# Expert blocks of at most 64 rows: the rests of x and h beside their nearest halves as stationary columns, and changes at two stage boundaries

## The reference

```python
h = h + hybrid_mixer(rmsnorm(h), ...)            # retention, SSD, S5; then w_out
h = h + cross_attend(rmsnorm(h), mn, wq, wk, wv, wo)
h = h + hier_moe(rmsnorm(h), ...)

def hier_moe(xn, ...):
    gsel = argmax(xn @ w_rg + b_rg)              # one of 4 groups of 8 experts
    top_p, top_i = top_k(softmax(elog of that group), 2)
    gate = pg * top_p / sum(top_p)
    # the 4096 pairs (token, expert) are sorted by expert, each expert's padded
    # to blocks of 128 rows; a block is computed with its expert's weights:
    h = silu(xb @ w_gate[e]) * (xb @ w_up[e]);   y = h @ w_down[e]
    # and y * gate is added to the token's row
```

## Time and profile before

| | us |
|---|---|
| time, three runs | 2474.22, 2474.22, 2477.82 (median 2474.22) |
| the profiled execution | 2471.07 |
| its span, first to last instruction | 2469.2 |
| granted TensorE clock, mean of the span | 0.968 |
| mixer stages | 0 to 924 |
| cross attention and router | 924 to 1558 |
| experts: routing and block 0 | 1558 to 1626 |
| experts: blocks 1 to 46 | 1626 to 2405 |

### The profile page before, as it was taken

The page is one execution under the profiler, slowest core; times in us unless marked ns, Lnnn a source line. Parts: engine busy times, 40 slices in busy tenths (PEclk is TensorE's granted clock), DMA queues, the critical chain, the costliest instruction groups (busy, mean ns, idle before and its releaser), DMA issues. The chain is left out here.

```text
span 2469.2 us, 34866 instructions
## 1 busy us (share of the span) xinstructions
PE 2267.5 (92%) x11995; PEld 1292.0 (52%) x11996; DVE 1407.6 (57%) x2052; ACT 987.0 (40%) x1418; POOL 368.0 (15%) x272
## 2 busy tenths in 40 slices
PE   4999999999979989999999999399999999999990
PEld 2465565565658974555555555145445445445440
DVE  5566566565569854333333332677556777777753
ACT  4522432433321333222222222246456666666653
POOL 0022021121220000000000000003222222122222
PEclk9999999999989999999999999599999999999995
DMA  5201001002050134111110100379777899988957
GB/s 196 90 2 50 35 26 61 1 26 45 9 213 26 52 123 142 52 60 44 69 69 35 60 35 35 138 261 319 233 241 252 292 313 319 333 311 301 320 185 287
DMA packets 150950, 349.50 MB, mean 142 GB/s; under 512 B 28480, under 2 KB 33984, under 8 KB 150592
## 3 DMA queue, kind: packets, MB, share of 16 engines
q1 hardware_dynamic: 136016, 310.32, 34.5%
q0 software_dynamic: 13680, 33.58, 5.8%
q10 hardware_dynamic: 1152, 4.19, 0.4%
HBM read 303.48 MB, written 60.82 MB: 148 GB/s over the span
## 5 line engine op out<-in xcount | busy, mean ns | idle before, releaser
L111 PE MATMUL bankA<-main_room,hnT 128*128 128x512 f16 (+1 forms) x1536 | 303.2, 356 | 5.5 <-DVE main_room L609 5.5
L111 PE MATMUL bankE<-wg,xT 128*128 128x512 f16 x1128 | 255.6, 384 | 7.9 <-DVE xT L2484 7.4
L111 PE MATMUL bankE<-wd,hT 128*128 128x512 f16 x1128 | 251.1, 379 | 2.4 <-DVE hT L2489 2.4
L111 PE MATMUL bankE<-wu,xT 128*128 128x512 f16 x1128 | 251.1, 379 | 0.0
L111 PEld LDWEIGHTS bankA<-main_room,hnT 128*128 128x128 f16 x1536 | 151.7, 99 | 148.7 <-issue 7.3
L111 PEld LDWEIGHTS bankE<-wg,xT 128*128 128x128 f16 x1128 | 111.2, 99 | 144.9 <-issue 15.3
L111 PE MATMUL bankA<-hnT,main_room 128*128 128x512 f16 x768 | 170.4, 384 | 9.0 <-DVE hnT L585 9.0
L111 PEld LDWEIGHTS bankE<-wd,hT 128*128 128x128 f16 x1128 | 110.2, 98 | 125.7 <-issue 3.0
L111 PEld LDWEIGHTS bankE<-wu,xT 128*128 128x128 f16 x1128 | 110.3, 98 | 122.9
L2461 DVE SCALAR_TENSOR_TENSOR wg<-w_rows,wg 128x2048 f16<-128x2048 f32 x64 | 143.8, 2288 | 49.9 <-ACT wg L2232 49.9
L111 PE MATMUL bankC<-w_out_s,catT 128*128 128x512 f16 x768 | 169.4, 381 | 2.5 <-DVE w_probs L1861 2.5
(11 more groups left out here) (373 smaller groups left out, 3275.1 us busy)
## 6 DMA issues: line engine op xcount, KB each, us to landing
w_rows<-in_w_gate SPq DMA_DIRECT2D x64, 1024.0 KB, 5.8
w_rows<-in_w_up SPq DMA_DIRECT2D x64, 1024.0 KB
w_rows<-in_w_down SPq DMA_DIRECT2D x64, 1024.0 KB
x_room<-in_x SPq DMA_DIRECT2D x4, 2048.0 KB, 11.0
cat_t<-scratch_cat SPq DMA_DIRECT2D x16, 512.0 KB, 4.9
main_room<-in_x SPq DMA_DIRECT2D x16, 512.0 KB, 5.6
scratch_ybuf<-main_room SPq DMA_DIRECT2D x16, 512.0 KB, 2.6
out<-hf SPq DMA_DIRECT2D x16, 512.0 KB, 11.9
```

The costliest lines, as they stand in the source:

```text
L111: ins = pe.matmul(o, a[x][k], b[y][k], start=start and k == 0 and j == 0, stop=stop and k == n - 1 and j == 2)
```

## The change

**Short blocks.** `plan` gets a row of numbers (PL_HALF): for the last block of an expert, if it is not the expert's first, has at most 64 rows and is neither block 0 nor the last of all, its number among such blocks, else 0. It is computed by nine more operations on DVE in the routing. For such a block `x_rest` and `h_rest` write the rest of the 64 columns that hold tokens into columns 64 to 127 of the nearest half's tile. `short_products` then takes two products for each k tile: all 128 columns (nearest and rest) by the weights' nearest, whose rows 64 to 127 are the rest's share, and the 64 nearest columns by the weights' rest. That makes 16 for 24. The two halves of rows are added afterwards: ACT copies rows 64 to 127 of the bank (`gate_low`, `up_low`, `y_lows`), DVE adds them (`gate_sum`, `up_sum`, `y_sums`). All three engines read the new number in each step and branch on it; `last` keeps the whole form.

**Routing.** The clearing of `xr` and `again` moves from DVE to POOL. The counting matmuls are in f16 with their constants converted on ACT, and the counts no longer depend on the scan's whole output; ranks are waited for apart. The six operations on gates move behind the first lists.

**Cross boundary.** `probs_weights(0)` moves to the end of `s5_mixer`, and the PSUM banks `vbank` are kept across the boundary, so that `VB` names eight banks; the load of a head's rows waits for one head less.

```diff
+def short_products(pe, o, a, b):
+    both, nearest = a
+    n = len(both)
+    for k in range(n):
+        turn = (False, True) if k == n - 1 else (True, False)
+        for full in turn:
+            if full:
+                ins = pe.matmul(o, both[k], b[0][k], start=k == 0, stop=k == n - 1)
+            else:
+                pe.matmul(o[0:P // 2, :], nearest[k], b[1][k], start=False, stop=False)
+    return ins
...
@@ s5_mixer, behind its last products
+            pe.wait_ge(begun.w_co_ld[0], 16)
+            pe.wait_ge(memory.w_lo, 2 * KT)
+            head = big[:, 0:2 * D].rearrange("p (k n) -> p k n", k=2)
+            for m in range(MT):
+                for j in range(2):
+                    for e in range(2):
+                        ins = pe.matmul(memory.bank[2 * m + j], values_t[:, e, m * P:(m + 1) * P], head[:, e, j * 512:(j + 1) * 512], start=(e == 0), stop=(e == 1))
+                    ins.then_inc(begun.vw_first, 1)
...
             def head(h):
-                if h >= 2:
-                    sp.wait_ge(vw_done, 4 * (h - 1))
+                if h >= 3:
+                    sp.wait_ge(vw_done, 4 * (h - 2))
...
-            probs_weights(0)
+            probs_weights(1)
             pe.wait_ge(ld, 16)
+            pe.wait_ge(vw_lo, 4)
             turn_cat(0)
-            probs_weights(1)
             probs_weights(2)
             probs_weights(3)
...
+        def short_block(eng, b):
+            return eng.value_load(plan[0:1, bass.ds(PL_HALF + 1 + b, 1)], min_val=0, max_val=NE)
...
@@ ACT
             def step(b):
                 take_h(b - 1)
-                silu(b)
+                h = short_block(act, b)
+                with act.If(h < 1):
+                    silu(b)
+                with act.If(h > 0):
+                    gate_low(b, h)
+                    silu(b)
+                    up_low(b)
                 following(act, b, gates(b))
                 take_x(b + 1)
                 following(act, b, ups_downs(b))
-                take_y(b - 1)
+                h = short_block(act, b - 1)
+                with act.If(h < 1):
+                    take_y(b - 1)
+                with act.If(h > 0):
+                    y_lows(b - 1)
...
-            dve.memset(xr[:, :], 0.0).then_inc(x_clear, 1)
-            dve.memset(again[:, :, :], 1.0).then_inc(ready, 1)
-            dve.wait_ge(ready, 1)
-            dve.memset(again[:, :, 0:1], 0.0).then_inc(ready, 1)
-            dve.wait_ge(ready, 2)
...
@@ DVE
             def step(b):
-                h_rest(b - 1)
+                y_sums(b - 2)
+                by_rows(b - 1, h_rest)
+                h = short_block(dve, b)
+                with dve.If(h > 0):
+                    gate_sum(h)
                 following(dve, b, gate_rest)
-                product(b)
-                x_rest(b + 1)
+                with dve.If(h < 1):
+                    product(b)
+                with dve.If(h > 0):
+                    up_sum(h)
+                    product(b)
+                by_rows(b + 1, x_rest)
                 following(dve, b, up_down_rest)
...
-            pe.matmul(bank[5][:, :], lt, flat(both), start=True, stop=False)
+            pe.matmul(bank[5][:, :], lt_h[:, :], flat(both), start=True, stop=False)
+            pe.matmul(bank[6][:, 0:NE], ones_h[:, :], both[:, :, NCH - 1], start=True, stop=False)
             pe.wait_ge(summed, 2)
-            pe.matmul(bank[5][:, :], ones, flat(before), start=False, stop=True)
-            pe.matmul(bank[6][:, 0:NE], ones, cum[:, :, NCH - 1], start=True, stop=True).then_inc(cnt, 1)
+            pe.matmul(bank[6][:, 0:NE], ones_h[:, :], before[:, :, NCH - 1], start=False, stop=True).then_inc(cnt, 1)
+            pe.matmul(bank[5][:, :], ones_h[:, :], flat(before), start=False, stop=True).then_inc(ranked, 1)
...
-            def by_slot(b, do):
+            def by_slot(b, do, whole=False):
                 u = expert_of(pe, b)
+                h = 0 if whole else short_block(pe, b)
                 for slot in range(SLOTS):
                     with pe.If(u % 2 < 1 if slot == 0 else u % 2 > 0):
-                        do(slot, u)
+                        if whole:
+                            do(slot, u)
+                        else:
+                            with pe.If(h < 1):
+                                do(slot, u)
+                            with pe.If(h > 0):
+                                do(slot, u, short_products)
```

More of the change, by code:

```diff
@@ L2072, in experts @@
         e32, pos = work(2, NCH, NGR, EPG), work(2, NCH, NE)
-        both, before, cum, again = (work(0, NE, NCH) for n in range(4))
+        cum, again = (work(0, NE, NCH) for n in range(2))
+        both, before = (sb(n, [P, NE, NCH], F16) for n in ("both", "before"))
+        lt_h, ones_h = sb("lt_h", [P, P], F16), sb("ones_h", [P, P], F16)
         E8, t8, m8, O8 = (work(0, NCH, EPG) for n in range(4))
@@ L2077, in experts @@
         nblk, first_blk, end, used_e, rank, eq, t32, first_row = (work(0, NE) for n in range(8))
-        cols, turns_f, first_f = work(0, 6), work(0, 1), work(0, 1)
-        c_expert, c_u, c_block, c_split, c_more, c_half = (cols[:, i:i + 1] for i in range(6))
+        cols, turns_f, first_f = work(0, 8), work(0, 1), work(0, 1)
+        c_expert, c_u, c_block, c_split, c_more, c_half, c_short, c_nth = (cols[:, i:i + 1] for i in range(8))
+        short_e = work(0, NE)
         lt, ones, one = cst[:, K_LT:K_LT + P], cst[:, K_ONE:K_ONE + P], cst[:, K_ONE:K_ONE + NE]
@@ L2167, in _ @@
         def _(pool):
+            pool.memset(again[:, :, :], 1.0).then_inc(ready, 1)
+            pool.wait_ge(ready, 1)
+            pool.memset(again[:, :, 0:1], 0.0).then_inc(ready, 1)
+            pool.memset(xr[:, :], 0.0).then_inc(x_clear, 1)
             pool.wait_ge(x_clear, 1)
@@ L2222, in _ @@
         def _(act):
+            act.activation(lt_h[:, :], lt, ACT.Copy).then_inc(lt_ready, 1)
+            act.activation(ones_h[:, :], ones, ACT.Copy).then_inc(lt_ready, 1)
             act.wait_ge(r_steps, env["r_marks"][0])
@@ L2254, in silu, with gate_low, up_low, y_lows @@
                 act.activation(sg[:, :], bank[2][:, :], ACT.Silu, scale=1.0 / (W_SCALE * X_SCALE)).then_inc(sil, 1)
+            def gate_low(b, h):
+                act.wait_ge(gd, b + 1)
+                act.activation(low[:, :], bank[2][HB:P, :], ACT.Copy).then_inc(g_low, 1)
+                act.wait_ge(g_sum, h)
+            def up_low(b):
+                act.wait_ge(ud, b + 1)
+                act.activation(low[:, :], bank[3][HB:P, :], ACT.Copy).then_inc(u_low, 1)
+            def y_lows(b):
+                act.wait_ge(y_t, b * 2)
+                act.wait_ge(y_st, b * 16)
+                for j, done in enumerate((yl0, yl1)):
+                    act.wait_ge(yd, b * 2 + j + 1)
+                    act.activation(y_low[:, j * 512:(j + 1) * 512], bank[5 + j][HB:P, :], ACT.Copy, scale=1.0 / (W_SCALE * H_SCALE)).then_inc(done, 1)
             def take_x(b):
@@ L2356, in _ @@
             dve.wait_ge(summed, 1)
+            dve.wait_ge(ready, 2)
             do(dve.tensor_tensor_scan, flat(cum), flat(again), flat(both), 0.0, ALU.mult, ALU.add)
@@ new lines, in y_sums, with rests @@
+            def y_sums(b):
+                h = short_block(dve, b)
+                with dve.If(h > 0):
+                    for j, done in enumerate((yl0, yl1)):
+                        js = slice(j * 512, (j + 1) * 512)
+                        dve.wait_ge(done, h)
+                        dve.scalar_tensor_tensor(y[0:HB, js], bank[5 + j][0:HB, :], 1.0 / (W_SCALE * H_SCALE), y_low[:, js], ALU.mult, ALU.add).then_inc(y_t, 1)
+            def rests(t, kk, short):
+                if short:
+                    return t[:, 0, kk, HB:P], t[:, 0, kk, 0:HB], slice(0, HB)
+                return t[:, 1, kk, :], t[:, 0, kk, :], slice(0, P)
@@ L2488, in h_rest, with by_rows @@
+            def h_rest(b, short=False):
+                o, near, cols = rests(hT, slice(0, FT), short)
                 dve.wait_ge(h_hi, b + 1)
-                dve.scalar_tensor_tensor(hT[:, 1, :, :], bank[4][:, :].rearrange("p (k n) -> p k n", k=FT), H_SCALE, hT[:, 0, :, :], ALU.mult, ALU.subtract).then_inc(h_lo, 1)
+                dve.scalar_tensor_tensor(o, bank[4][:, :].rearrange("p (k n) -> p k n", k=FT)[:, :, cols], H_SCALE, near, ALU.mult, ALU.subtract).then_inc(h_lo, 1)
+            def by_rows(b, do_rest):
+                h = short_block(dve, b)
+                with dve.If(h < 1):
+                    do_rest(b)
+                with dve.If(h > 0):
+                    do_rest(b, True)
@@ L2597, in products_of @@
                     for j in range(2):
-                        products(pe, bank[5 + j][:, :], [[hT[:, h, n, :] for n in range(FT)] for h in range(2)],
+                        products(pe, bank[5 + j][:, :], split(hT, FT, products),
                                  [[wd[:, slot, h, n, j * 512:(j + 1) * 512] for n in range(FT)] for h in range(2)]).then_inc(yd, 1)
```

110 lines of the change are left out of this document (73 added, 37 removed).

## The result

The changed kernel takes 2514.88 us (median; 2507.22 to 2519.84), the kernel before 2474.22: ratio 1.0161, 95% interval 1.0149 to 1.0174. It is 1.6% slower. The forecast was 2462 with a range of 2436 to 2484, so sign and range were wrong. The profiled execution of the changed kernel has a span of 2517.8, 48.6 more than the one before. The medians lie only 40.7 apart: the profiled execution after is the slowest of its four, and the one before lies 3.15 under its median. So some 8 of the 48.6 are spread between executions.

A forecast was written before the change was run, and what follows sets the result against it. The prediction took PE, busy in 92% of the span, as the bound, with chains on other engines just in time. Loop -8.1, cross -2.2 and routing -1.7 gave -12.0, so 2462 us from the median; range 2436 to 2484.

The forecast's parts named there:

- Does a 64-column product cost as much: Short groups' products: a change between 128 and 64 columns taken as 0, bound 0.10 us at each of 16 changes.
- The rival with this price: Short groups: each width change costs 0.10 us, groups take 5.05, total 2486 to 2492; chance 0.11.
- Short steps: Expert loop, 13 steps with a short block: fewer gate and up products bring the next gate earlier, -26.0 us.
- The y sums: DVE in the loop: sums ahead of the rest of h cost 1.4 in four steps, +5.6 us.
- Control on ACT and PE: Expert loop, 30 steps that convert weights: new reads and branches delay ACT's chain and PE, +12.3 us.
- The slack of PE: PE's control before the gate: 0.5 us spare in single rounds, 0.8 at the back edge of double ones.
- ACT's chain: Expert loop: ACT and DVE work up to x's rest has about 0.5 us of slack in steps that convert weights.
- The steps that wait for the rest of h: Short-block steps: down waits for DVE's rest of h, starting at T+9.4, with the next gate at T+14.5 to T+15.25.
- the rival on code: Expert loop: longer code must be fetched anew, one case of control costing more, 2471 to 2484; chance 0.22 together.
- Cross: Cross boundary: first head's products move into PE's idle time, first output product earlier, -2.2 us (bounds -8.8 and +0.5).
- Routing: DVE's routing chain: memsets on POOL and a shorter wait for counts, less new operations, -1.7 us (bounds -4 and +1).
- control up to +10: Expert loop: reads don't overlap as assumed, conversion steps cost 0.7 to 1.2 each, 2471 to 2484; chance 0.22.

The follow-up runs named there:

- run 2: Changed kernel with the product by the weights' rest taking all 128 columns, so a group has one width: 2493.74 us.
- run 3: Changed kernel with whole down products for short blocks again, without the y sums, their copies and their reads: 2481.42 us.
- run 11: Kernel before with two unused reads of the plan added on PE ahead of each product group: 2495.38 us.
- run 12: Kernel before with two unused reads of the plan added on ACT between the h copy and silu: 2489.15 us.
- run 5: Kernel before with the cross boundary part of the change alone: ratio 1.0001 (0.9992 to 1.001).
- run 1: Changed kernel with no block short, all reads, branches and both boundary changes kept: 2493.88 us.
- runs 4, 8 and 14: Changed kernel with the edits of run 2 and run 3, 2458.76 us; then run 8, 2450.44; on that, PE's expert and flag in one plan entry, 2448.02.
- run 8: Changed kernel with one width and whole down products, and ACT's read of the block's number moved ahead of the h copy: 2450.44 us.

## Why the prediction was wrong, point by point

- **"Does a 64-column product cost as much": the step that failed first.** I had the row with 0.32 for 0.22, wrote the bound of 0.10 for each change, and took 0, because products of one width behind it ran evenly. That says nothing on changes. The measured cost is 0.11 in the mean, in both directions, shown by the rows above and by run 2, where the spacing is even again. There are 14 changes in a gate or up group and 12 in a down group, not 16. The Trainium skill ("TensorEngine Tiling (Array Packing)", § Key Properties) says that a change of the tiling mode drains TensorE. The trace agrees so far that each change of width costs 0.11 us; that it is a drain, or that a 64-column product counts as such a change, no run here shows. The rival with this price gave 2486 to 2492, +12 to +18 over before. The profile's 48.6 without the long steps (28.9) and step 1 (3.3) is +16.4, so this rival had that part about right. Short steps, forecast at -26.0 with +5.6 for the y sums, came to -1.2; with one width (run 2) they came to -23.3.
- **"The y sums": the term with a missing queue.** I priced them at 1.4 on DVE where the rest of h is late (+5.6). On DVE they do what I said: the rest of h is at T+9.5 to T+9.6 in those steps. It delays nothing in the changed kernel, where down starts at T+11.4 anyway, and with one width down starts at T+10.5 there. But POOL's add waits for them, and POOL's gather stands behind the add; neither is in the sum. In place of 5.6 it was 29 in the long steps of the profiled run, and 33.5 went by the medians when the sums, the short down products and their reads went (run 3). The row for it was there: POOL's adds of the kernel before took 2664 ns in the mean and gathers 1755, and the shortest near 1.6 and 1.0.
- **Control on ACT and PE: right in the sum, less so in the parts.** The 30 conversion steps were forecast at +12.3 and came to +15.0; their kinds at 17.46, 17.03 and 17.64 for 17.1, 17.2 and 17.6. Behind short blocks it was twice the forecast and behind whole ones in double rounds half of it, so some of the agreement is luck. (The +3.0 for the nine steps there should have been 9 x 0.41 = 3.7 by its own price.) The slack of PE (0.5 and 0.8) gave +21 for run 11, which measured +21.0. ACT's chain gave +21 (13 to 24) for run 12, +14.8 measured: the x rest is not late by all of the 1.2.
- **The steps that wait for the rest of h: right in kind.** With one width (run 2) down starts at T+8.2 to T+8.6 in seven of the 13 and the next gate at T+13.5 to T+14.9, earlier than forecast (9.4 and 14.5 to 15.3); in the four with y sums it is 10.5 and 15.7 to 16.1, and at block 30 it is 11.4 and 18.0.
- **The first entry into the loop** cost 3.3 and is in no term: step 1 does not stand in the sum. PE waits 3.06 there, once, for nothing that the profile shows; if it is the code, that much of the rival on code is true. The wait has a sequel that the table counts with the conversion steps: step 2 takes 18.96, and its gate runs at a granted clock of 0.67 (1651 to 1656).
- **Cross:** -2.2 forecast, -0.5 in the profile from the stage's start to the first output product and 0 by run 5. The load was the bound as said; the lower clock behind the wait took more than the 1.7 I had: 6.48 for 8 products, where 3.45 is the higher level's time, so 3.0.
- **Routing:** -1.7 forecast, -0.2 in the profile (68.46 for 68.63 from the first reduce or memset to block 1's gate). The two gains came (-1.67, -2.1), and an operation that the change only retyped took 1.3 more, which I had at nothing.
- **The rivals.** Those on the slower side were held apart and priced one at a time: width +12 to +18, control up to +10. They don't exclude each other. The first came true; of the second, which wanted 0.7 to 1.2 for each conversion step, 0.5 came in run 1 and besides it the wait at the first entry. The cause of the long steps, POOL, was on no list. 0.60 for faster was far too high with a rule and a row both against the central zero.

## What to carry to other kernels

A measured odd spacing at just the pattern that a change will repeat forty times a block is a price, not a bound: use one tile width in a group, even if half the rows then compute something small and useless. When an operation moves from one engine to two, follow its semaphore to every queue that waits for it, the gather and scatter queue above all, and look at what stands behind it there. Saving work on the engine that is busy 100% gives little while chains on others run 0.5 us behind it; shortening those (a read ahead of a wait, two numbers in one entry) gave back 10.7 us (runs 4, 8 and 14, on three chips).

## What the runs showed of the hardware

- A change between 128 and 64 stationary columns costs 0.11 us (0.31 to 0.34 for 0.2155), both ways, f16, 512 moving columns, at clock 1.00. Weight loads of 64 columns took 0.106 and those of 128 columns 0.096.
- POOL's indirect DMA (1.04 for a gather, 1.59 for an add when alone) doesn't finish under a DVE conversion from f32 to f16 (128x2048). In 13 of these traces 369 gathers that start under one end 0.87 to 0.93 after the end of a conversion, and 335 adds 1.45 to 1.50 after it. Mostly that is the conversion they start under, in 33 adds the second of a pair, and in four gathers, all of the changed kernel, the fourth (9.8 us). Only some that start within 0.03 us of a conversion's start get through in their own time.
- One read of the plan costs 0.5 to 0.6 us of an engine's control: two more on ACT put its conversion 1.07 later (run 12, 2.71 for 1.64 behind whole blocks), and the read moved ahead of the wait for h gives 0.61 back (run 8).
- The sum `both` (128x512, written through a strided pattern) took 2.32 us as f16 and 1.02 as f32, one operation in each profile.
- After a wait of 5.1 us PE ran at the lower clock level, 8 f32 products in 6.48 for 3.45 at a granted clock of 0.55.
